# Four of eleven down-projection units by seven block products, with two sets of weight sums, and moved pieces in both attention phases

## What is computed

```python
def swiglu(x, w_gate, w_up, w_down):
    return (jax.nn.silu(x @ w_gate) * (x @ w_up)) @ w_down      # 1024 -> 2816 -> 1024
...
for layer in range(DEPTH):
    h = h + 0.5 * swiglu(rms_norm(h, ln_ffn1[layer]), ...)
    u = rms_norm(h, ln_mix[layer])
    h = h + diff_attention(u, ...)            # layer 0; layer 1: swa_sink_attention
    h = h + 0.5 * swiglu(rms_norm(h, ln_ffn2[layer]), ...)
return rms_norm(h, final_norm)
```

## Time and profile before

| | us |
|---|---|
| median of three runs | 910.48 (910.34 to 911.45) |
| the profiled execution, its own time | 910.87 |
| its span, first to last instruction | 909.1 |
| PE busy | 897.9 (99%) |
| DVE busy | 671.1 (74%) |
| ACT busy | 496.6 (55%) |
| POOL busy | 95.5 (11%) |

### The profile page before, as it was taken

One profiled execution on the slowest core, in us unless ns is written; L12 is line 12 of the kernel. 1 busy time (PEld: TensorE's weight loads), 2 busy tenths in 40 slices (PEclk: granted clock), 3 DMA queues, 4 the chain that ended last, 5 costly groups with the idle time before them and its releaser, 6 DMA issues.

```text
span 909.1 us, 11935 instructions
## 1 busy us (share of the span) xinstructions
PE 897.9 (99%) x4159; PEld 739.0 (81%) x4159; DVE 671.1 (74%) x908; ACT 496.6 (55%) x663; POOL 95.5 (11%) x170
## 2 busy tenths in 40 slices
PE   8999999999999999999999999999999999999997
PEld 7888888888887888888888888888877788888885
DVE  5666779774787768777887577788788776876884
ACT  6455446365685645445545454554578664445641
POOL 1100005824311100000002000000030000000000
PEclk9999999999999999999999999999999999999999
DMA  9897778758733788776747878777563388987631
GB/s 310 253 305 242 243 233 215 254 182 290 243 93 93 233 271 277 249 254 223 237 138 225 250 247 250 255 239 259 187 232 108 124 265 269 272 253 256 212 138 47
DMA packets 169759, 202.87 MB, mean 223 GB/s; under 512 B 15160, under 2 KB 139136, under 8 KB 169712
## 3 DMA queue, kind: packets, MB, share of 16 engines
q1 hardware_dynamic: 168752, 201.37, 68.1%
q0 software_dynamic: 512, 0.36, 0.7%
q10 hardware_dynamic: 448, 0.53, 0.2%
HBM read 184.39 MB, written 17.83 MB: 222 GB/s over the span
## 4 chain that ended last, share of the span: by engine, by line
PE 91%; DVE 4%; DMA 2%; issue 1%; ACT 1%; SPq 1%; POOL 0%; POOLq 0%; DVEq 0%; ACTq 0%
PE bank L576 59%; PE bank L618 14%; PE bank L625 7%; PE bank L641 2%; PE bank L640 2%; PE bank L642 2%; PE bank L682 2%; PE bank L855 1%; PE bank L725 1%; DVE w_lo L1887 1%; PE bank L886 1%; DMA raw<-in_ffn_w_up 1%; DMA x_bounce<-h 0%; PE bank L908 0%; PE bank L832 0%
## 5 line engine op out<-in xcount | busy, mean ns | idle before, releaser
L1887 DVE TENSOR_TENSOR w_lo<-raw,w_hi 128x2048 fp32r<-128x2048 f32 x149 | 338.8, 2290 | 102.5 <-ACT w_hi L1476 102.1
L1476 ACT ACTIVATE w_hi<-raw 128x2048 fp32r<-128x2048 f32 x154 | 294.1, 1915 | 126.1 <-PE bank L576 64.8
L576 PE MATMUL bank<-w_hi,xT_hi 128*128 128x512 f32 x816 | 318.9, 391 | 0.2 <-DVE w_lo L1975 0.2
L576 PE MATMUL bank<-w_lo,xT_hi 128*128 128x512 f32 x816 | 317.6, 389 | 0.0
L576 PE MATMUL bank<-w_hi,xT_lo 128*128 128x512 f32 x816 | 307.9, 389 | 0.0
L576 PEld LDWEIGHTS bank<-w_hi,xT_hi 128*128 128x128 f32 x816 | 153.2, 188 | 32.9 <-DVE w_lo L1975 0.6
L576 PEld LDWEIGHTS bank<-w_hi,xT_lo 128*128 128x128 f32 x816 | 153.2, 188 | 32.0
L576 PEld LDWEIGHTS bank<-w_lo,xT_hi 128*128 128x128 f32 x816 | 153.2, 188 | 31.4
L618 PE MATMUL bank<-w_hi,hT_hi 128*128 128x512 f32 x252 | 98.2, 390 | 0.0
L618 PE MATMUL bank<-w_lo,hT_hi 128*128 128x512 f32 x252 | 98.0, 389 | 0.0
L1547 ACT ACTIVATE hT_hi<-xn 128x512 f32 (+1 forms) x40 | 25.0, 625 | 100.8 <-DMA xn<-h_bounce 100.8
(11 more groups left out here) (225 smaller groups left out, 893.6 us busy)
## 6 DMA issues: line engine op xcount, KB each, us to landing
raw<-in_ffn_w_down SPq DMA_DIRECT2D x88, 512.0 KB, 4.7
raw<-in_ffn_w_gate SPq DMA_DIRECT2D x86, 512.0 KB, 5.5
raw<-in_ffn_w_up SPq DMA_DIRECT2D x86, 512.0 KB, 6.7
raw<-in_a_w_qkv SPq DMA_DIRECT2D x24, 512.0 KB, 5.9
h_bounce<-silu SPq DMA_DIRECT2D x40, 256.0 KB, 6.4
xn<-h_bounce SPq DMA_DIRECT2D x160, 64.0 KB, 3.4
xn<-x_bounce SPq DMA_DIRECT2D x64, 64.0 KB, 2.0
raw<-in_a_w_o SPq DMA_DIRECT2D x8, 512.0 KB, 5.0
```

Source lines behind the costliest of these rows:

```text
L576: mm = nc.tensor.matmul(bank[b][:, :], xs[:, kt, own(pos)], ws[:, slot(u), cols], start=(kt == 0 and i == 0), stop=(kt == KT - 1 and i == 2))
L1476: nc.scalar.activation(w_parts(u)[0], raw[:, slot(u), :], ACT.Copy).then_inc(s_hi, 1)
L1887: nc.vector.tensor_tensor(lo, raw[:, slot(u), :], hi.bitcast(F32), ALU.subtract).then_inc(s_lo, 1)
```

## The change

- `SEVEN` becomes d2, d4, d5, d6: in each feed-forward block a fourth down unit takes seven block products. `DN_ORDER` is changed so that its hidden blocks fit.
- The hidden sums of the fourth one (`n` = 3) are made in `turn_of(4)`, on DVE after `mul(0, 0)`, into `last_sums_raw`, `last_sums_hi` and `last_sums_lo`, which lie on other buffers (`junk`, `rot`).
- The T buffers become two sets of three parts of 128x1536 over `xT_hi`, `xT_lo`, `silu` and `h`, which now lie next to each other; set `n % 2` serves unit `n`. T sums of unit `n` wait for PE's use of unit `n - 2`; those of `n` = 1, whose set lies on `silu` and `h`, wait for the transfers that read these.
- The calls of the down stage stand in a new order on DVE and ACT. Low parts are written over the raw sums.
- Layer 0 attention: the transposes of `x` for pos 0 stand before `wo(0, 1)`, the later bank first. Layer 1: `wo(2, 0)` is cut in two, the first half after `scores(1, 1, 2)`; DVE splits its unit in halves; the last `scaled` moves to ACT, DVE keeps its reciprocal; maxima of round 3 are taken in two steps around `scaled(1, 2)`.

```diff
@@ -85,8 +85,8 @@
-DN_ORDER = [1, 3, 0, 5, 2, 6, 4, 7, 8, 9, 10]
-SEVEN = [2, 4, 6]
+DN_ORDER = [1, 3, 0, 5, 2, 4, 6, 7, 8, 9, 10]
+SEVEN = [2, 4, 5, 6]
 N_SEVEN = len(SEVEN)
 SEVEN_END = SEVEN[-1] + 1
...
+        T_FLOATS = 2 * KT * SEQ + 4 * NPOS * CH
+        with nc.sbuf_tensor("t_raw", [P, T_FLOATS], F32) as t_raw:
+            pass
+        with nc.sbuf_tensor("t_split", [P, T_FLOATS], F32R) as t_split:
+            pass
         xT_hi = sb("xT_hi", [P, KT, SEQ], F32R)
-        with nc.sbuf_tensor("t_raw", [P, KT * SEQ], F32) as t_raw:
-            pass
         xT_lo = sb("xT_lo", [P, KT, SEQ], F32R)
+        silu = sb("silu", [P, NPOS, 2, CH])
+        h = sb("h", [P, NPOS, 2 * CH])
         with nc.sbuf_tensor("att_1", [P, FT * SEQ], F32) as att_1:
...
+            pass
+        with nc.sbuf_tensor("last_sums_lo", [P, BANK], F32R) as last_sums_lo:
+            pass
         junk = sb("junk", [P, D], BF16)
...
-        t_hi = xT_hi[:, :, :].rearrange("p k s -> p (k s)")
-        t_lo = xT_lo[:, :, :].rearrange("p k s -> p (k s)")
+        def t_of(view, n, part):
+
+            at = (2 * (n % 2) + part) * 3 * BANK
+            return view[:, at:at + 3 * BANK]
+
+        def h_sums_of(n, part, turn=None):
+
+            if n == N_SEVEN - 1:
+                return (last_sums_hi, last_sums_lo)[part][:, :]
+            if turn is None:
+                return h_sums[:, n, part, :]
+            return h_sums[:, bass.ds(turn, 1), part, :].rearrange("p o n -> p (o n)")
+
+        def h_sums_raw(n, turn=None):
+
+            if n == N_SEVEN - 1:
+                return last_sums_raw[:, :]
+            return vec[:, bass.ds(turn, 1), BANK:D].rearrange("p o n -> p (o n)")
         kvb = shared[:, 0:512].rearrange("p (t n) -> p t n", t=NPOS)
...
-                if pos == 0 and (u, part) == (U_WO_A + 3, 0):
-                    pe.wait_ge(s_wo_half, 1)
+                if pos == 0 and part == 0 and u in (U_WO_A + 3, U_WO_B + 2):
+                    pe.wait_ge(s_wo_half, (U_WO_A + 3, U_WO_B + 2).index(u) + 1)
                 elif pos == 0:
...
                 values(1, 2)
                 values(1, 3)
+                x_transposes("wo", 0, js=(1, 0))
                 wo(0, 1)
-                x_transposes("wo", 0)
...
-                def wo(i, pos):
-                    projected(1, U_WO_B, i, pos)
+                def wo(i, pos, part=None):
+                    projected(1, U_WO_B, i, pos, part)
                 turned_values(0, 0)
...
+                wo(2, 0, 0)
                 p_transposes(1, 1, 1)
                 turned_values(1, 0)
                 scores(1, 1, 3)
                 turned_values(1, 1)
-                wo(2, 0)
+                wo(2, 0, 1)
                 p_transposes(1, 1, 2)
                 wo(0, 1)
                 p_transposes(1, 1, 3)
...
                 act.wait_ge(s_t_sums, seven_no(f, n))
-                nc.scalar.activation(t_hi[:, 0:3 * BANK], t_raw[:, 0:3 * BANK], ACT.Copy).then_inc(s_t_hi, 1)
-
-            def h_sums_high(f, turn):
-
-                act.wait_ge(s_h_sums, turn + seven_no(f, 0))
-                nc.scalar.activation(h_sums[:, bass.ds(turn, 1), 0, :], vec[:, bass.ds(turn, 1), BANK:D],
-                                     ACT.Copy).then_inc(s_h_sums_hi, 1)
+                nc.scalar.activation(t_of(t_split, n, 0), t_of(t_raw, n, 1), ACT.Copy).then_inc(s_t_hi, 1)
+
+            def h_sums_high(f, n, turn=None):
+
+                if (f, n) == (2, N_SEVEN - 1):
+                    act.wait_ge(s_kdup, 2)
+                act.wait_ge(s_h_sums, seven_no(f, n) if turn is None else turn + seven_no(f, 0))
+                nc.scalar.activation(h_sums_of(n, 0, turn), h_sums_raw(n, turn), ACT.Copy).then_inc(s_h_sums_hi, 1)
...
-                        h_sums_high(f, turn)
+                    if turn is not None or g == 4:
+                        h_sums_high(f, g - 1, turn)
                 def first_turn():
...
+                split(u0 + 25)
                 t_high(f, 0)
-                split(u0 + 25)
                 split_with_t1(u0 + 26, f, 1)
+                t_high(f, 1)
                 h_hi(1, 4)
-                split(u0 + 27)
-                t_high(f, 1)
-                split_with_t1(u0 + 28, f, 2)
+                split_with_t1(u0 + 27, f, 2)
+                t_high(f, 2)
+                split_with_t1(u0 + 28, f, 3)
+                t_high(f, 3)
                 h_last_hi(0)
                 h_last_hi(1)
-                split(u0 + 29)
-                t_high(f, 2)
-                for i in range(30, 33):
+                for i in range(29, 33):
...
                 copy_bank(dst, b, s_filled, filled[key]).then_inc(s_read[b], 1)
+
+            def scaled(pos, r):
+
+                n = per_bank(pos)
+                p = probs[r % 2].rearrange("p (i c k) -> p i c k", i=n, c=2)
+                act.wait_ge(s_last_rden, 1)
+                act.wait_ge(s_exp, exp_count(1, pos, r, 1))
+                for c in range(2):
+                    for i in range(n):
+                        ins = nc.scalar.activation(p[:, i, c, :], p[:, i, c, :], ACT.Copy,
+                                                   scale=rden[:, pos, n * r + i, c:c + 1])
+                    ins.then_inc(s_scaled, 1)
             def exps(layer, pos, r, cs=(0, 1)):
...
             o_hi(1, 1, 0)
             exps(1, 1, 3)
+            scaled(1, 3)
             p_transposed(1, 1, 2)
...
                     dve.wait_ge(s_used, u - SEVEN[0])
+                elif n == 1:
+                    for pos in range(NPOS):
+                        dve.wait_ge(s_bounced[pos], block_no(f, H_BLOCKS - 1) * 16)
+                        dve.wait_ge(s_last_bounced[pos], (f + 1) * 16)
                 else:
-                    dve.wait_ge(s_t_used, seven_no(f, n) - 1)
+                    dve.wait_ge(s_t_used, seven_no(f, n - 2))
                 dve.wait_ge(s_t1, seven_no(f, n))
-                t2, t4, t3 = [t_raw[:, BANK * i:BANK * (i + 1)] for i in range(3)]
+                t2, t4, t3 = [t_of(t_raw, n, 1)[:, BANK * i:BANK * (i + 1)] for i in range(3)]
                 link(nc.vector.tensor_tensor(t2, raw_tile(u, 0, 1), raw_tile(u, 1, 1), ALU.add))
                 nc.vector.tensor_tensor(t4, t2, raw_tile(u, 1, 0), ALU.add)
                 nc.vector.tensor_tensor(t3, t2, raw_tile(u, 0, 0), ALU.subtract).then_inc(s_t_sums, 1)
...
                                         ALU.subtract).then_inc(s_t_lo, 1)
-            def h_sum(f, turn):
...
                     mul(0, 0)
-                    if turn is not None:
-                        h_sum(f, turn)
+                    if turn is not None or g == 4:
+                        h_sum(f, g - 1, turn)
                     if turn is not None:
                         dve.wait_ge(s_h_sums, turn + seven_no(f, 0))
-                    a_copied(0)
-                    if turn is not None:
-                        h_sum_low(f, turn)
+                    if g < 4:
+                        a_copied(0)
+                    if turn is not None or g == 4:
+                        h_sum_low(f, g - 1, turn)
...
                 t_sums(f, u0 + 24, 0)
                 t_first(f, u0 + 26, 1)
+                split(u0 + 25)
                 t_low(f, 0)
-                split(u0 + 25)
+                t_sums(f, u0 + 26, 1)
                 split(u0 + 26)
-                t_sums(f, u0 + 26, 1)
+                t_low(f, 1)
+                t_first(f, u0 + 27, 2)
+                split(u0 + 27)
+                t_sums(f, u0 + 27, 2)
                 h_lo(1, 4)
-                t_first(f, u0 + 28, 2)
-                t_low(f, 1)
-                split(u0 + 27)
+                t_first(f, u0 + 28, 3)
+                t_low(f, 2)
+                t_sums(f, u0 + 28, 3)
                 split(u0 + 28)
-                t_sums(f, u0 + 28, 2)
+                t_low(f, 3)
+                split(u0 + 29)
                 h_last_lo(0)
                 h_last_lo(1)
-                t_low(f, 2)
-                for i in range(29, 33):
+                for i in range(30, 33):
                     split(u0 + i)
                 seven_added(f)
-            def maxima(layer, pos, r):
+            def maxima(layer, pos, r, cs=(0, 1)):
                 n, keys = per_bank(pos), P * (pos + 1)
...
             o_lo(1, 0, 1)
+            split_half(U_WO_B + 2, 0)
             scaled(1, 1)
-            split(U_WO_B + 2)
             heads_maxima(1, 2)
-            heads_maxima(1, 3)
+            split_half(U_WO_B + 2, 1)
+            maxima(1, 1, 3, (0,))
             scaled(1, 2)
+            maxima(1, 1, 3, (1,))
+            sink_minus_max(1, 3)
             o_lo(1, 1, 0)
-            scaled(1, 3)
+            reciprocals(1, 3).then_inc(s_last_rden, 1)
             split(U_WO_B + 3)
             next_phase(1, U_FFN2_1, "ln_ffn2_1")
```

(3 more changed lines are left out.)

48 lines of the change are left out of this document (25 added, 23 removed).

## The result

The changed kernel takes **918.49 us** (median of 4 runs, 918.24 to 919.5) against 910.97 us (median of 4, 910.34 to 911.72) in the same session: ratio 1.0088, 95% interval 1.0076 to 1.0101. It is slower, as forecast, and inside the range of 915.0 to 922.5; the forecast was 919.9 us. Its profiled span is 916.6 us, 7.5 us more than the 909.1 us before.

What follows compares the result with a forecast made beforehand. PE, 99% busy, sets the time, but DVE, 89% busy from d2 to d6, would make it wait. Down projections +10.5, attention −0.9 and −0.2 give +9.4: 919.9 us against 910.48, range 915.0 to 922.5.

Steps and rivals of the forecast that it cites:

- The bound: Whole kernel: PE, 99% busy, sets the time, but DVE, 89% busy from d2's to d6's begin, decides the case.
- Rival 1: Down stages: DVE keeps up, so PE's saving of 2.7 us and attention's 1.1 come through, 906.7 us; chance 0.08.
- DVE idles for 2 us here: Down stage, block f = 1: DVE's gap before the split of d5, as ACT's part lies between T1 and split.
- Waits in block f = 1: PE waits for DVE's T low part at d2, d5, d6: 0.8, 1.0, 1.0 us; less 0.68 saved, 2.14 lost.
- The other blocks, +1.94 us: Blocks f = 0, 2, 3: `mul(0, 0)` is less far ahead of d0 than f = 1's 3.80 us, adding 1.24, 0.32, 0.38.
- Sum of the down projections: Four feed-forward blocks: 4 x 2.14 + 1.94 = +10.5 us; 9.7 to 11.7 with the bounds of the hidden sums.
- rival 3: DVE's T sums of d4: `h_last_bounce` lands late and delays DVE and PE; 924 with 1 us per block; chance 0.08.
- Attention: Layer 0: PE's 0.88 us wait for the bank of `wo(0, 1)` goes, −0.9; layer 1: −0.2, bounds −0.6 and +0.4.

Runs made afterwards that it cites:

- the mended one: Changed kernel with DVE's down-projection instructions in another order, nothing else changed: 907.82 us, ratio 0.9965; with attention 1 also as before the change: 906.83 us, 0.9953.

## Why the prediction was right, point by point

- *The bound.* The prediction held that DVE, at 89% in the stretch of the seven-product units, decides. It does; that was the right view to open. But the share itself is not the cause: 88% in the changed kernel goes with waits, 97% in the mended one with none. What decides is when the chain over DVE and ACT reaches T low.
- *Rival 1, PE's saving comes through (906.7 us).* It did not in the changed kernel. The mechanism that the prediction gave for its failing was incomplete: it put the lateness on the work added in front and never asked what the idle times cost. Its own working names the gap at d5 ("DVE idles for 2 us here") and the row for d2's, and takes them as given. With the order mended the rival's number about comes true: 906.83 to 907.82 us for 906.7. The room was there: DVE's work from d2's to d6's begin is 19.08 us in the mended kernel for 18.20 before, in 19.72 us.
- *Waits in block f = 1.* Predicted 0.8, 1.0 and 1.0 us, measured 0.58, 0.90 and 0.94. T1 was put 3.0 us behind `mul(0, 0)` and came at 2.84; from T1 to the split 2.79 was taken and 2.73 measured. From `mul(0, 0)` to d6 the sum was 448.45 − 411.23 = 37.22 us and is 36.99. In four blocks the sum is 0.9 us too large.
- *The other blocks, +1.94 us.* This term failed. It took the lead as a property of the block (2.56, 3.80, 3.48, 3.42, together 13.26 us). Only for f = 0 is that near the truth (2.35 to 3.30 us in all the traces): the same blocks in the changed kernel have 2.88, 3.76, 3.86 and 4.51, together 15.01. That is 1.75 us of the error. What moves it is the low part of `h` that DVE makes just ahead of `mul(0, 0)`. It waits for ACT's high part, and ACT for the transfer back from `h_bounce`: ACT stands idle for 4.20 us in f = 0 of the changed kernel and for 2.57 in f = 3, DVE behind it for 1.59 us and not at all. DVE's wait and the lead add up to 4.47 us in f = 0, 1 and 2. Block f = 0:

```profile
124.87 0.63 ACT L1574 ACTIVATE hT_hi<-xn 128x512 fp32r<-128x512 f32 x1 [4.20 <-DMA xn<-h_bounce]
...
125.53 0.69 DVE L2122 TENSOR_TENSOR hT_lo<-xn,hT_hi 128x512 fp32r<-128x512 f32 x1 [1.59 <-ACT hT_hi L1574]
```

- *Sum of the down projections.* Predicted +10.5, measured by d6 2.83 + 1.95 + 1.91 + 1.22 = +7.9 us. The two terms above, 0.9 and 1.75, are the difference. The sum of the whole was too large by less, 9.4 for 7.5 us, because other errors go the other way: above all, the stretch between the third and the fourth block, with attention 1 in it, is 0.6 us longer in the changed kernel's trace by what d6 does not explain, where −0.2 was forecast. That the total fell so near the forecast is in part luck.
- *Transfers, rival 3.* No wait of DVE at the T sums of d4 ends with a transfer. It cost nothing, as taken.
- *Attention.* Predicted −0.9 and −0.2; measured −1.0 and 0. The wait of 0.88 us is gone; `wo(0, 1)` follows its transposes at once, and nothing is late behind it. For attention 1 the prediction weighed a fitting half split against a later scaling, and missed that PE's own cover was moved.
- *Rules of the pages.* The Trainium skill ("Perfetto Trace Analysis", "Identifying the Most-Contended Engine") has the engine with the highest occupancy optimized first. PE had 99% (its weight loads, by which that section would judge TensorE, had 81%, still the most), it got 12 matmuls fewer, and the time rose by 7.5 us. With the order mended the same 12 matmuls did come through, so the engine was rightly chosen; the rule by itself does not tell that a second engine loses its cover on the way. The other rule ("VectorE: DVE Perf Modes", "The DRAIN you can't avoid"), of semaphores that cost nothing in a chain, does not hold in these rows either: behind an add whose semaphore DVE waits for, the next begins 0.32 us later, behind one without such a wait 0.22 us. These are the four hidden sums of n = 3, f = 1; the first two are linked:

```profile
413.38 0.28 DVE L1966 TENSOR_TENSOR last_sums_raw<-shared 128x128 f32<-128x128 f32 x1
413.70 0.29 DVE L1967 TENSOR_TENSOR last_sums_raw<-shared,last_sums_raw 128x128 f32<-128x128 f32 x1
414.02 0.29 DVE L1968 TENSOR_TENSOR last_sums_raw<-shared 128x128 f32<-128x128 f32 x1
414.24 0.28 DVE L1969 TENSOR_TENSOR last_sums_raw<-shared,last_sums_raw 128x128 f32<-128x128 f32 x1
```
